# Column sums of the modulation vector: fp32 products against pairs of fp32r products

## The reference, cut to what matters

```
def adaln(cvec, w_mod, b_mod):
    return jnp.split(jax.nn.silu(cvec) @ w_mod + b_mod, 6, axis=-1)

sh1, sc1, gt1, sh2, sc2, gt2 = [m[:, None] for m in adaln(c, w_mod[l], b_mod[l])]
csh1, csc1, cgt1, csh2, csc2, cgt2 = adaln(c_ctx, w_mod[l], b_mod[l])
h = modulate(rmsnorm(x, g_pre1[l]), sh1, sc1)
...
x = x + gt1 * rmsnorm(y, g_post1[l])
h2 = modulate(rmsnorm(x, g_pre2[l]), sh2, sc2)
x = x + gt2 * rmsnorm(conv_ffn(h2, w_up[l], conv_w[l], conv_b[l], w_down[l]), g_post2[l])
```

## Time and profile before

| what | value |
|---|---|
| median of three runs | 1456.22 us |
| lowest and highest | 1455.99 and 1457.41 us |
| the profiled execution | 1457.66 us |
| its span, first to last instruction | 1455.8 us |
| PE busy | 1376.8 us, 95% of the span |
| DVE busy | 842.8 us, 58% |
| ACT busy | 630.4 us, 43% |
| mean granted clock of TensorE | 0.975 of full speed |

### The profile page before, as it was taken

How to read it: one execution, slowest core, us unless ns; L and a number is a source line. 1 busy time by engine, 2 the same in 40 slices (tenths; PEclk the granted TensorE clock), 3 DMA queues, 4 the chain that set the end, 5 groups by cost and what they waited for, 6 DMA issues and landing times.

```text
span 1455.8 us, 16898 instructions
## 1 busy us (share of the span) xinstructions
PE 1376.8 (95%) x6720; PEld 1110.6 (76%) x6720; DVE 842.8 (58%) x1247; ACT 630.4 (43%) x1006; POOL 39.7 (3%) x34
## 2 busy tenths in 40 slices
PE   7989978897999999999999999999989999999995
PEld 5767656575888888888896777797868888888885
DVE  5575767538776766766755544347375453344335
ACT  5345545543545544333642554444454333334333
POOL 3000000003001300000000000000000000000000
PEclk9999988998999999999999999999999999999998
DMA  6423211032322322466121111222204432322321
GB/s 228 178 88 129 75 57 43 23 138 98 108 97 87 102 94 94 165 227 215 59 97 58 59 44 58 73 102 89 88 27 134 141 130 87 102 93 96 101 87 59
DMA packets 45610, 146.69 MB, mean 101 GB/s; under 512 B 4795, under 2 KB 11963, under 8 KB 45148
## 3 DMA queue, kind: packets, MB, share of 16 engines
q1 hardware_dynamic: 45388, 145.08, 29.5%
q10 hardware_dynamic: 144, 0.52, 0.1%
HBM read 142.18 MB, written 3.41 MB: 100 GB/s over the span
## 4 chain that ended last, share of the span: by engine, by line
PE 80%; DVE 10%; ACT 6%; issue 3%; DMA 2%; SPq 0%; DVEq 0%; ACTq 0%
PE PS L330 24%; PE PS L331 23%; PE PS L332 23%; DVE wlo L296 1%; DVE X L1605 1%; PE PS L986 1%; ACT L L1124 1%; ACT whi L285 1%; PE PS L977 1%; DVE mt L1599 1%; DVE G_b L1599 1%; DVE Z L1605 1%; PE PS L951 1%; PE PS L607 1%; PE PS L524 1%
## 5 line engine op out<-in xcount | busy, mean ns | idle before, releaser
L296 DVE TENSOR_TENSOR wlo<-raw,whi 128x1024 fp32r<-128x1024 f32 x206 | 252.6, 1233 | 387.5 <-ACT whi L285 387.4
L330 PE MATMUL PS<-Hhi,whi 128*128 128x512 f32 (+1 forms) x1104 | 432.7, 392 | 31.6 <-DVE wlo L296 9.9
L331 PE MATMUL PS<-Hlo,whi 128*128 128x512 f32 (+1 forms) x1104 | 422.0, 382 | 0.0
L332 PE MATMUL PS<-Hhi,wlo 128*128 128x512 f32 (+1 forms) x1104 | 421.6, 382 | 0.0
L285 ACT ACTIVATE whi<-raw 128x1024 fp32r<-128x1024 f32 x206 | 216.1, 1055 | 262.3 <-DMA raw<-in_w_down 118.3
L330 PEld LDWEIGHTS PS<-Hhi,whi 128*128 128x128 f32 x1104 | 211.9, 192 | 86.8 <-issue 19.3
L332 PEld LDWEIGHTS PS<-Hhi,wlo 128*128 128x128 f32 x1104 | 211.5, 192 | 40.1
L331 PEld LDWEIGHTS PS<-Hlo,whi 128*128 128x128 f32 x1104 | 212.1, 192 | 38.0 <-issue 1.0
L330 PE MATMUL PS<-Dhi,whi 128*128 128x512 f32 (+1 forms) x384 | 142.9, 372 | 0.0
L331 PE MATMUL PS<-Dlo,whi 128*128 128x512 f32 (+1 forms) x384 | 142.6, 371 | 0.0
L332 PE MATMUL PS<-Dhi,wlo 128*128 128x512 f32 (+1 forms) x384 | 142.6, 371 | 0.0
(11 more groups left out here) (382 smaller groups left out, 1826.2 us busy)
## 6 DMA issues: line engine op xcount, KB each, us to landing
raw<-in_w_up SPq DMA_DIRECT2D x88, 512.0 KB, 3.5
wm<-in_w_mod SPq DMA_DIRECT2D x48, 512.0 KB, 3.7
raw<-in_w_down SPq DMA_DIRECT2D x44, 512.0 KB, 3.5
raw<-in_w_g SPq DMA_DIRECT2D x16, 512.0 KB, 3.5
raw<-in_w_out SPq DMA_DIRECT2D x8, 512.0 KB, 3.4
raw<-in_w_o SPq DMA_DIRECT2D x8, 384.0 KB, 3.3
raw<-in_w_sq SPq DMA_DIRECT2D x4, 512.0 KB, 4.3
raw<-in_w_sk SPq DMA_DIRECT2D x4, 512.0 KB, 4.4
```

Of the source, the lines that this page charges most:

```text
L296: e.tensor_tensor(wlo[i % NS], raw[i % NS], whi[i % NS].bitcast(f32), ALU.subtract).then_inc(q["w_lo"], 1)
L330: e.matmul(o, lhs[0], rhs[0], start=first, stop=False, skip_group_check=own)
L331: e.matmul(o, lhs[0], rhs[1], start=False, stop=False, skip_group_check=own)
L332: return e.matmul(o, lhs[1], rhs[0], start=False, stop=last, skip_group_check=own)
```

## The change

Each group's sum (g = 4 to 11) is split like every other operand: ACT writes its fp32r high part (`mod_hi`), DVE the low part in place of the sum (`mod_lo`), and `acc_columns` takes, for each 128 outputs, two fp32r products with a moving operand of two columns of ones, in place of one fp32 product with one column. Groups below 4 are as they were. The edits to the programs of the engines:

```diff
+    ones2 = at("ones2", "K", kk + 4864 + 960, [128, 2], f32r)
+    mhi = at("mhi", "A", 32768, [128, 6, 512], f32r)
+    mhi2 = at("mhi2", "E", 0, [128, 2, 512], f32r)
+    mlo4 = at("mlo4", "E", 0, [128, 4, 512], f32r)
+    mlo2 = at("mlo2", "P", 8192, [128, 2, 512], f32r)
...
+    def mod_hi(e, g):
+        e.wait_ge(q["mod_acc"], MOD_OPS[4 * g + 4])
+        if g < 10:
+            e.wait_ge(q["dd_lo"], 16 + g - 4 + 1)
+        e.activation(mod_halves(g)[0], mod_sum(g, 0), mybir.ActivationFunctionType.Copy).then_inc(q["m_hi"], 1)
+
+    def mod_lo(e, g):
+        hi, lo = mod_halves(g)
+        e.wait_ge(q["m_hi"], g - 3)
+        e.tensor_tensor(lo, mod_sum(g, 0), hi.bitcast(f32), ALU.subtract).then_inc(q["m_lo"], 1)
...
         def acc_columns(g, bank, at):
+            if g >= 4:
+                e.wait_ge(q["m_lo"], g - 3)
+                e.wait_ge(q["ones2"], 1)
+                for n in range(4):
+                    o = PS[:, bank, at + 2 * n:at + 2 * n + 2]
+                    hi, lo = mod_halves(g)
+                    e.matmul(o, hi[:, 128 * n:128 * n + 128], ones2, start=True, stop=False)
+                    last = e.matmul(o, lo[:, 128 * n:128 * n + 128], ones2, start=False, stop=True)
+                last.then_inc(q["mcol"], 1)
+                return
...
(ACT, down)
                 split_to(i0 + f + AHEAD)
+                if layer == 0 and f == 0:
+                    act(ones2, ones[:, 0:2], ACT.Copy, "ones2")
+                if layer == 0 and f in (18, 19):
+                    mod_hi(e, 2 * f - 32)
+                    mod_hi(e, 2 * f - 31)
             split_to(i0 + NF - 2 + AHEAD)
+            if layer == 0:
+                mod_hi(e, 8)
+                mod_hi(e, 9)
...
(ACT, second up projection)
+            if n in (23, 24):
+                mod_hi(e, n - 13)
...
(DVE, down)
                 split_to(i0 + f + AHEAD)
+                if layer == 0 and f in (18, 19):
+                    mod_lo(e, 2 * f - 32)
+                    mod_lo(e, 2 * f - 31)
             split_to(i0 + NF - 2 + AHEAD)
+            if layer == 0:
+                mod_lo(e, 8)
+                mod_lo(e, 9)
...
(DVE, second up projection)
+            if n in (24, 25):
+                mod_lo(e, n - 14)
```

More of the change, by code:

```diff
@@ L91, in build @@
     small = at("small", "K", kk + 4864, [128, 240])
-    assert kk + 4864 + 960 <= 7744
+    assert kk + 4864 + 960 + 8 <= 7744
     def vc(name, i=0, n=1):
@@ L310, in mod_sum, with mod_halves @@
         return macc4[:, g - 4, :] if 4 <= g < 8 else macc[:, v if g < 4 else g % 2, :]
+    def mod_halves(g):
+        hi = mhi[:, g - 4, :] if g < 10 else mhi2[:, g - 10, :]
+        return hi, mlo4[:, g - 4, :] if g < 8 else mlo2[:, g % 2, :]
+    def mod_hi(e, g):
[7 more added lines that the diff above has]
+        e.tensor_tensor(lo, mod_sum(g, 0), hi.bitcast(f32), ALU.subtract).then_inc(q["m_lo"], 1)
     def mod_load(e, n):
```

## The result

The changed kernel takes 1459.39 us (median of 20 runs, 1454.39 to 1462.32) against 1456.41 us of the kernel before on the same chips (20 runs). The ratio is 1.0020, with a 95% interval from 1.0012 to 1.0028: 3.0 us slower, with an interval from 1.7 to 4.1. The forecast was +1.2 us, so the sign was right and the size too small. The median lies inside the range of 1453.8 to 1461.0, but above the forecast's own band (to 1458.5) and just past the 1459.1 from which I had counted it as slower, a case that I had given 0.16; at 0.20% it stands on the edge of what I had called no change. Measured once more later, the ratio was again 1.0020 (1.0011 to 1.0028).

The account below looks back on a forecast made before the run. PE, busy for 95% of the span, was taken to bound the kernel. Between-blocks delay +1.20, PE 0 and clock 0 sum to +1.2 us: 1456.22 + 1.2 = 1457.4 us, range 1453.8 to 1461.0.

Parts of the forecast that it names:

- the forecast's own band: Total time between 1456.5 and 1458.5 us, by bounds of +-0.9 us for PE; chance 0.50.
- a case that I had given 0.16: Whole kernel slower by over 0.2%, above 1459.1 us: a new clock fall, or four instructions in series with PE loss.
- PE's term, 0: Column products on PE's path: eight fp32r loads cost what eight fp32 loads cost, so 0 us gained.
- The bounds of 0.9 us to either side: PE's 48 records on the path: 0.9 us won or lost if loads go at 0.101 or 0.12 us.
- Both ways in which the pair would be cheaper: Column products: half the passes, 2.9 us lower; or faster fp32r loads, 1451.2 to 1454.5 us, chance 0.08.
- Between the blocks, 1.20 us: Before PE's first product of block two: two activations and two subtractions delay ACT and DVE; 1.20 us stay.
- "PE's new wait, for the low part, is met 10 us or more ahead": PE's wait for DVE's low part before the pairs: already met when PE arrives, so costing nothing.
- "I expect the fall to stay": Columns of g = 6 to 9: clock still falls to 0.50, about 3.3 us lost as before, so 0 change.
- the rival by which the clock holds up: Columns of g = 6 to 9: clock fall gone or shorter, 3.3 us come back, 1454.1 us; chance 0.14.
- The rival that ends slower: New clock fall between the blocks from a gap 1.2 us longer: 3.3 us lost, 1460.7 us; chance 0.13.
- my three signs of being wrong: Chunk-to-product distance (22.3 us forecast) does not grow, pairs take less time than old products, or clock falls at other places.

Follow-up runs that it names:

- the run with both moves: Changed kernel with splits of g = 10 and 11 one chunk earlier and those of g = 8 and 9 moved from between the blocks: 1456.28 us, 1.0004 to kernel before.
- the move of the splits: Changed kernel with splits of g = 8 and 9 moved from between the blocks to behind the second half's norm: 1459.37 us, 1.0027 to kernel before.
- the kernels with the delay but without the wait: Changed kernel with splits of g = 10 and 11 one chunk earlier (1.0008, again 0.9988), or PE taking g = 11 one chunk later (1.0001); ratios to kernel before.

## Why the prediction was right in sign and short in size

*PE's term, 0: right.* Eight loads stayed eight loads, 1.90 us for sixteen in both kernels, and the run with both moves has the time of the kernel before (1.0004, 0.9995 to 1.0012). The bounds of 0.9 us to either side were wide enough. Both ways in which the pair would be cheaper are out. That it is loads that count holds for these narrow products alone: an fp32 product of 512 columns (`permc`, line 903) leaves two records that PE passes in 755.49 to 756.35, 0.86 us, against 0.23 us from one fp32r product of that width to the next.

*Between the blocks, 1.20 us: right in mechanism.* The two subtractions push the first sum of squares by 1.20 us, and the move of the splits took 1.22 us off the stage. A pause of 0.35 us on DVE went away at the same time, which no step foresaw, so 0.87 us reached PE. In the total these cannot be told: the kernels with the delay but without the wait came out at 1.0008, 0.9988 and 1.0001. So the right sign is luck: the part that I had summed does not show in the time, and what made the kernel slower is a part that I had left out.

*"PE's new wait, for the low part, is met 10 us or more ahead": wrong, and this is the step that failed.* It holds for g = 4 to 9. For g = 10 the low part ends at 1209.0 and PE takes it at 1212.6 (first profile), 3.6 us ahead; for g = 11 it comes 1.8 us late. I had asked whether ACT and DVE have idle time in that stage, and they have. I had not asked when the idle time lies: DVE's lies ahead of a chunk's low part, whose data are on their way, and the subtraction stands behind it and behind two instructions of the convolution. What is queued ahead of the instruction that ends a new wait I had followed for ACT, and for DVE only between the blocks. The numbers were there: a chunk and one group on PE are 6.1 us, the path from the DMA's issue to the low part 3.4 + 1.1 + 1.2, and behind it 1.4 + 0.6, in all 7.9 us with the gaps, by the chain above. The two DVE lines of the kernel before give the same 1.7 us.

*The clock: "I expect the fall to stay".* Behind g = 9 it did in one profile of the changed kernel, for 3.4 us at half speed. In the second profile the clock holds through the pairs, which end at 759.5, and falls later:

```profile
756.00:760.00 4.00, 4.00 (x36) 3.92 (x35) 2.42 (x7) 2.05 (x3) 0.00 (x0) 1.00 0.58 217
760.00:764.00 4.00, 4.00 (x20) 3.28 (x19) 4.00 (x4) 1.98 (x2) 0.00 (x0) 1.00 0.01 4
776.00:780.00 4.00, 2.26 (x6) 1.80 (x7) 3.13 (x6) 0.76 (x3) 0.00 (x0) 0.79 0.00 1
780.00:784.00 4.00, 4.00 (x14) 2.88 (x13) 0.77 (x2) 1.72 (x5) 0.00 (x0) 0.78 0.02 4
```

This fall comes behind 2.4 us in which PE stood idle, until 777.7, and costs (0.21 + 0.22) x 4 = 1.7 us, as much as that of the first profile. So the rival by which the clock holds up came true by half at most in these profiles, 1.7 of its 3.3 us. The rival that ends slower had named a new fall, but between the blocks and for a longer gap there; the new fall came behind the wait that I had missed, and costs 1.7 us. Of my three signs of being wrong one came true, a fall of the clock at another place. The missed step is worth 1.8 + 1.7 = 3.5 us; the time falls into the stated range only because that range had been drawn for another fall.

*What stays open.* 3.5 us for the wait and its fall and 0.87 us between the blocks make 4.4 us; measured were 3.0 (1.7 to 4.1). Between 750 and 790 us the clock cost the profiled execution before 3.4 us and each of the two of the changed kernel 1.7; 4.4 - 1.7 = 2.7 us would close the gap. But the three profiles of the kernels that have the changed program up to that place lost 5.1, 5.1 and 1.7 us there, and the two of the kernel with only the last two groups changed, which has the old program there, 3.4 and 5.1. What the clock takes in that stretch varies from one execution to the next by more than the gap, so the gap is not explained.

## What to carry to other kernels

Idle time on an engine covers an added instruction only if it lies behind that instruction in program order: find what the engine is waiting for when it idles, and whether the consumer needs the result before that arrives. A product of one or two columns cost its weight load here, so pairs in its place gained nothing; putting such products into PE's idle time, or group by group between full products, gained 0.35% and 0.23%. Where a short wait is added to a PE-bound stage beside nearly empty products, look at the clock behind it too: here the wait of 1.8 us brought a second loss of 1.7.

## What the hardware showed that I had not expected

Four fp32 products of one column and four pairs of fp32r products of two columns take the same time, eight loads about 0.11 us apart. The granted clock fell to half with PE recorded as 100% busy, during or just behind 4 us of such products, in nine of ten profiles, and setting the same products apart won 0.23% (0.13 to 0.33). With a pause of 1.8 us between two groups of them another fall followed in all five profiles, and none in the seven without the pause. And DVE had a pause of 0.35 us at one instruction, in every kernel in which its program was unchanged up to there, and in none in which four or six instructions had been put in earlier.
